# Attention steps: a product stage that ends closes its step's filler, and a second score product moves behind the filler

## What is computed

```python
br = split_projection(h @ lw['w_in'])           # q, k, v, gates of branches A and B; u, v, gate of C
a_out = dense_gqa(qa, [ka, ka_ctx], [va, va_ctx])       # softmax over latent and cached keys
b_out = window_gqa(qb, kb, vb, kb_ctx, vb_ctx, sink)    # |i-j| <= 128, plus cached keys and a sink logit
c_out = u * mixed(layer_norm(v))
ya = (a_out * silu(br['ga'])) @ w_proj_a        # the same for b and c
y  = (sigmoid(h @ w_gate)_a * ya + ..._b * yb + ..._c * yc) @ w_out
x  = layer_norm(ALPHA * x + gate * y)
```

## Time and profile before

| | us |
|---|---|
| median of 3 runs | 1410.67 |
| lowest, highest | 1410.13, 1411.56 |
| profiled execution, first to last instruction (page) | 1406.3 |
| PE busy in it | 1353.3 (96%) |
| DVE, ACT, POOL busy | 769.7, 623.7, 693.0 |

### The profile page before, as it was taken

How to read it: one execution, slowest core, us unless ns; L and a number is a source line. 1 busy time by engine, 2 the same in 40 slices (tenths; PEclk the granted TensorE clock), 3 DMA queues, 4 the chain that set the end, 5 groups by cost and what they waited for, 6 DMA issues and landing times.

```text
span 1406.3 us, 22404 instructions
## 1 busy us (share of the span) xinstructions
PE 1353.3 (96%) x8624; PEld 1252.1 (89%) x8624; DVE 769.7 (55%) x1605; ACT 623.7 (44%) x1298; POOL 693.0 (49%) x500
## 2 busy tenths in 40 slices
PE   6998999999999999999999999999999999999997
PEld 4898989899888999999877988998989989999985
DVE  5756773263873511656694577722458715036557
ACT  4436876234764211213254478852367733222230
POOL 3455565334665354344663566642256554445453
PEclk9999999999999999999999999999999999999999
DMA  9312001122012244354321210012111042225321
GB/s 374 125 61 80 16 31 46 61 88 67 31 46 98 98 165 151 104 210 136 120 101 39 91 61 31 31 46 79 61 61 45 31 135 67 70 76 195 131 79 76
DMA packets 36762, 126.94 MB, mean 90 GB/s; under 512 B 5040, under 2 KB 5680, under 8 KB 36656
## 3 DMA queue, kind: packets, MB, share of 16 engines
q1 hardware_dynamic: 29952, 108.54, 22.5%
q10 hardware_dynamic: 6704, 16.97, 3.3%
HBM read 119.73 MB, written 5.77 MB: 89 GB/s over the span
## 4 chain that ended last, share of the span: by engine, by line
PE 86%; DVE 6%; POOL 3%; ACT 2%; issue 2%; DVEq 0%; POOLq 0%; ACTq 0%
PE ps L939 50%; PE ps L887 6%; PE ps L889 6%; PE ps L888 6%; PE ps L1082 4%; PE ps L1072 3%; PE ps L1074 2%; PE ps L1093 2%; PE ps L1094 2%; DVE x L1745 1%; PE ps L956 1%; POOL with_eps L1764 1%; POOL w_lo L1780 1%; POOL p_f_a L1806 1%; POOL rstd L1765 1%
## 5 line engine op out<-in xcount | busy, mean ns | idle before, releaser
L1780 POOL TENSOR_TENSOR w_lo<-raw,w_hi 128x1024 fp32r<-128x1024 f32 x148 | 361.9, 2452 | 265.3 <-ACT w_hi L1137 182.4
L939 PE MATMUL ps<-h_hi,w_hi 128*128 128x320 f32 x1280 | 295.7, 312 | 8.7 <-DVE g_c L1685 4.6
L939 PE MATMUL ps<-h_hi,w_lo 128*128 128x320 f32 x1280 | 292.0, 309 | 0.0
L939 PE MATMUL ps<-h_lo,w_hi 128*128 128x320 f32 x1280 | 291.5, 309 | 0.0
L939 PEld LDWEIGHTS ps<-h_hi,w_hi 128*128 128x128 f32 x1280 | 218.0, 188 | 25.4 <-DVE g_c L1685 6.0
L1137 ACT ACTIVATE w_hi<-raw 128x1024 fp32r<-128x1024 f32 x148 | 154.1, 1055 | 145.1 <-DMA raw<-in_weights 67.3
L939 PEld LDWEIGHTS ps<-h_hi,w_lo 128*128 128x128 f32 x1280 | 215.1, 188 | 1.8
L939 PEld LDWEIGHTS ps<-h_lo,w_hi 128*128 128x128 f32 x1280 | 215.2, 188 | 1.6
L887 PE MATMUL ps<-w_hi,h_hi 128*128 128x512 f32 (+1 forms) x360 | 129.3, 359 | 2.1 <-POOL w_lo L1780 2.0
L889 PE MATMUL ps<-w_hi,h_lo 128*128 128x512 f32 (+1 forms) x360 | 127.6, 354 | 0.0
L888 PE MATMUL ps<-w_lo,h_hi 128*128 128x512 f32 (+1 forms) x360 | 127.5, 354 | 0.0
(11 more groups left out here) (182 smaller groups left out, 2615.5 us busy)
## 6 DMA issues: line engine op xcount, KB each, us to landing
raw<-in_weights SPq DMA_DIRECT2D x190, 512.0 KB, 3.3
raw_more<-in_weights SPq DMA_DIRECT2D x10, 512.0 KB, 10.5
x<-in_x_sample ACTq DMA_DIRECT2D x6, 512.0 KB, 9.8
x_mid<-x ACTq DMA_DIRECT2D x5, 512.0 KB, 2.6
x<-x_mid ACTq DMA_DIRECT2D x5, 512.0 KB, 6.0
y_sample<-x SPq DMA_DIRECT2D x3, 512.0 KB, 2.6
pack<-in_pack ACTq DMA_DIRECT2D x2, 528.0 KB, 6.2
x<-in_x_sample SPq DMA_DIRECT2D x2, 512.0 KB, 5.1
```

The lines of the kernel that those rows point to most:

```text
L939: last = pe.matmul(ps[:, s + half, 0:HALF], w[:, u % RING, cols], acts[:, k, half * HALF:(half + 1) * HALF], start=k == 0 and part == 0, s ...
L1780: did(pool.tensor_tensor(w_lo[:, n % RING, :], raw_tile(r), w_hi[:, n % RING, :], ALU.subtract), w_ready)
```

## The change

Two edits in `attention`.

```diff
     def fill():
         used[0] += 1
         upto = len(filler) * used[0] // places
-        out.extend(filler[used[1]:upto])
-        used[1] = upto
+        while used[1] < upto:
+            out.append(filler[used[1]])
+            used[1] += 1
+            if isinstance(filler[used[1] - 1][0], tuple) and used[0] < places:
+                break
...
     for n, (g, i) in enumerate(steps):
         out.append(("T", l, br, g, i))
-        out.extend(scores[n])
+        out.extend(scores[n][:1])
         out.append(("pl", l, br, g, i))
         out.extend(inverses[n])
         tick()
         if n >= lag:
             product(n - lag)
         fill()
+        out.extend(scores[n][1:])
         out.extend(exps[n])
```

## The result

The changed kernel takes 1419.37 us (median of 4 runs, 1417.74 to 1420.31) where the kernel before takes 1411.12 us on the same chip: a ratio of 1.0055 [1.0042, 1.0068], 8.3 us slower. The direction of the forecast and the chains that it named hold, the size does not: 4.2 us were forecast, and the time lies 0.6 us above the range.

What follows compares the result with a forecast made beforehand. PE, busy 96% of the span, was taken as the bound, so only its waits in branch B counted. Layer losses of 2.0 and 2.3 less 0.1 gave 4.2 us: 1410.67 + 4.2 = 1414.9 us, range 1408.0 to 1418.8.

Steps and rivals of the forecast that it cites:

- The waits are covered, and chains take their place: Branch B: five PE waits, 5.53 us in layer 0, get covered, but delayed scores' chains return as waits of T.
- The first place: S(1,3) and c1's first chunk in branch B: T(1,0) reached sooner, then waits 2.15 us for POOL.
- Part 2: Start of branch B, S(1,3) and c1's first chunk: two idle sites become one wait of T(1,0), gain nothing.
- Part 3: Middle of branch B: S(2,3)'s mask starts at about 359.4, T(2,0) waits 0.5, PE 0.8 us behind from T(2,3).
- Part 4: u1's first chunk in branch B: T(5,3) at its old time, balance 0; S(7,3) then gives 0.6 net before T(6,2).
- Part 5: End of branch B: S(9,0) behind two chunks, its exponentials at 428.4, not 426.41; chain ends 2.0 us later.
- the formula: End of branch B: u3's first chunk starts 15.94 us after T(6,2) plus the wait at u2, where it was 14.41.
- Part 6: The rest: layer 1 loses 2.3 us, branch A 0, small waits rounded up by 0.1; total 4.2 us.
- What is added to the span is added to the median: Whole kernel: profiled span of 1406.3 us lies 4.4 under the median 1410.67; additions to one carry to the other.
- The rival for "slower by more": Branch B: later second scores of groups 3 to 5 overrun the slack of T(3,0), T(4,0) or T(5,0); 1421, chance 0.07.
- The rule weighed there: PE's drain waits: rotating independent matmul groups through PSUM banks would end all named waits, 10.7 us, giving 1400.0.

Runs made afterwards that it cites:

- e5: Changed kernel with eight unused matmuls filling T(1,0)'s wait in branch B of both layers; 1417.98 us.
- e6: e5 with the tg of c0 moved directly ahead of pl(1,0) on DVE in branch B; 1414.05 us.
- e3: Changed kernel with S(9,0) back directly behind S(8,0) in both branches; 1415.70 us.
- e11: Changed kernel with S(7,3) and S(9,0) back directly behind the scores in front of them; 1415.19 us.
- before_again: The kernel before, unchanged, run once more for a second profile; 1413.04 us, span 1411.2.
- e9: Kernel before with e8's covers, and the first chunks of u1 and u3 one step later, behind T and PV; 1404.83 us.
- e2: Kernel before with the second edit alone: second scores behind PV and chunks, chunks where they were; 1421.30 us.
- e8: Kernel before, branch B: a chunk ahead of S(1,3), the PV ahead of S(2,3) and S(7,3), DVE's order kept; 1409.34 us.
- e1: Kernel before with the first edit alone: a step stops taking chunks after a pair, scores stay together; 1412.29 us.

## Why the prediction was right and wrong

**The waits are covered, and chains take their place: right.** The first place behaved as worked out: T(1,0) waited 2.09 us for POOL (forecast 2.15). The branch has 1.9 us more of idle time, and the forecast, which knew only waits, had 2.0. That these sums agree is partly chance: in e5 the work between T(1,0) and T(1,1) takes 1.45 us less and the branch only 0.43, so without the slow clock PE would have waited some 1.0 us more.

**Part 2, "gain of the first two places: nothing": wrong in what that wait sets off.** The sum took PE's own durations for given, the clock at 1.00. Behind the wait it fell to half for 3.4 us, in both layers: from T(1,0) to T(1,1) PE took 5.11 us, where e5 takes 3.66. e5 shows the price at the end, 0.43 and 0.25 us a layer, because T(2,0) would have waited anyhow.

**Part 3, "PE 0.8 us behind from T(2,3) on": the term that failed most.** It was 2.09. The prediction had S(2,3)'s mask start at 359.4, 28.7 us behind the branch's start; it came at 29.46. The step "behind pl, two iv and a tg" took the tg at its 0.82 us, and it took 1.57, since the iv in front had just started POOL's multiplication. e6 ends the layers 1.02 and 1.05 us sooner, but of the 1.04 us at the mask 0.28 are idle time that it fills on DVE; by that share, an estimate from e5's and e6's rows, the longer tg costs some 0.8 us a layer. The trace of before held a warning: there a tg that starts 0.16 us ahead of a POOL product takes 0.81, and the product 1.54 us where the four of the earlier trace rows take 1.01 each (DVE's and POOL's rows of before):

```profile
384.35 0.81 DVE L1678 SCALAR_TENSOR_TENSOR g_c<-gate_tanh,g_c 128x640 f32<-128x640 f32 x1
```

```profile
384.51 1.54 POOL L1806 TENSOR_TENSOR p_f_b<-p_f_b,inv 128x512 f32<-128x512 f32 x1 [1.14 <-DVE inv L1658]
```

At its old place c0's tg met no POOL instruction, and the change put it 0.15 us behind one:

```profile
355.15 0.82 DVE L1678 SCALAR_TENSOR_TENSOR g_c<-gate_tanh,g_c 128x640 f32<-128x640 f32 x1
```

With both effects away e6 ends the layers at +2.15 and +2.29, forecast 2.0 and 2.3. That it fits so closely is partly luck: without the 0.28 us that e6 gains besides, about +2.4 and +2.6 would stand there (an estimate), and the small waits forecast at S(3,2), S(3,3) and c2's first chunk, 0.4 us, are in no row of the changed kernel.

**Part 4, u1: size off.** From T(2,3) to T(5,3) 0.8 us were to come back and 0.35 did (0.33 in e6). Then T(6,2) another 0.73 sooner, forecast 0.58.

**Part 5, the formula: right; the cause given for it: half right.** T(6,2) to u3's first chunk was forecast at 15.94 plus the wait at u2, 1.05; it was 17.01, with S(9,0)'s first exponential 7.73 us behind T(6,2) (forecast 7.7). But of the 2.6 us only 1.4 come back with S(9,0) (e3). The other 1.2 come from S(7,3), whose iv hold up the drain of u1, and this S(8,0)'s maximum (e11). The prediction saw that drain as a wait of u2's chunk, not as what stands ahead of S(8,0) on DVE: without the one the other remains. And S(7,3) put back meets the late S(7,1).

**Part 6.** Layer 1 was to lose 0.3 more; it lost the same. In the sum the branches give 7.2 us, forecast 4.3; what e5 and e6 take back, parts 2 and 3, makes up 2.8 of these 2.9 us. What the medians show beyond 7.2 us isn't resolved. "What is added to the span is added to the median" holds only for executions with the same start. The 4.4 us between the first profile's span and the median of the kernel before are no fixed distance: every run with both has 1.8 us between its time and its span (1413.04 and 1411.2 for `before_again`), so the first profile was of an execution faster than the median, the one with the short start. And u3's first chunk stands in the loop, behind T(8,0), not past it; neither edit of the change moves it, so nothing hung on that. The rival for "slower by more", 1421, comes nearest in time, but for another reason: in the changed kernel T(3,0), T(4,0) and T(5,0) wait for nothing.

**The rule weighed there** (Trainium skill, "Perfetto Trace Analysis"), independent groups that rotate so that a drain overlaps matmuls, gave 1400.0. e9, which covers waits without moving anything on DVE, shows that it points the right way: 1404.83. e2, which moves scores on DVE too, loses 4.87 us a layer. It also moves seven more scores than e8, so that DVE's order alone turns the gain into a loss is argued and not shown. And e1, which moves no score, loses 1.55 us by taking the chunk away from in front of T(1,0).

## What to carry to other kernels

Cover a wait with work that only the waiting engine does, and keep the order of the others: where one list orders all engines, moving a score past a wait on PE also moves its maximum behind pl and iv on DVE, and in this kernel that chain is what PE waited for next. Ask too what the moved work had covered in its old place, and what is tied to it, as the tg is to its chunk. Look at who starts first where two engines hold each other up; a change of order can turn a delay of the one with slack into a delay of the one without. And look at the granted clock behind a new wait, not at its length alone; what a fall costs at the end depends on the waits that follow.

## What the hardware showed

**DVE and POOL hold each other up, and the later one pays.** tg alone or 0.16 us ahead of a POOL product: 0.81 us; 0.15 us behind one: 1.57, in both layers of the changed kernel and of e1. The POOL product pays when it is second: 1.54 us for 1.01. The Trainium skill, "SBUF — State Buffer", section "Who interferes with whom", says that a DVE instruction with two inputs in SBUF and a GpSimd instruction that reads SBUF contend, and that issue order decides who blocks. Of DVE's two-port modes it says that whoever issues first holds the shared pair for the whole instruction. tg has two inputs in SBUF. If the first holds on to its end here too, tg should have lost the 0.86 us that were left of a product of 1.01; the trace has 0.75 more, and for the product 0.53 more where 0.65 of tg were left. Direction and order agree, the sizes are 0.1 us smaller.

**The granted clock falls behind waits of this size, but not behind each.** It was at half for 3.4 us behind a wait of 2.09 us (changed kernel), of 2.22 us (e2) and of 0.37 and 1.42 us close together (e1). It stayed at 1.00 behind 1.60 us of idle PE at u1 in the kernel before, 1.41 us at u3 in the changed one and 1.36 us at S(7,3) in e11. Which waits do it can't be told from these rows. Filled with matmuls, the same place kept 1.00 (e5, both layers).
